# Making the prompt's keys and values between the last steps of the sample attention, with single waits in place of a meeting

## The reference

```python
q_lat = jnp.einsum("bthn,chn->bthc", q[..., :QK_NOPE], lw["w_uk"])
ckv = rmsnorm(ckv, lw["kv_norm_g"])
...
s = (einsum("bqhc,bkc->bhqk", q_lat, ckv) + einsum("bqhr,bkr->bhqk", q_pe, kpe)) * MLA_SCALE
s = where(k_pos <= q_pos, s, -inf)
o_lat = einsum("bhqk,bkc->bqhc", softmax(s), ckv)
yb = jnp.einsum("bthc,chv->bthv", o_lat, lw["w_uv"]).reshape(B, T, 512)
```

## Time and profile before

| | |
|---|---|
| median of 3 runs | 2403.9 us (2401.56 to 2406.0) |
| the profiled execution's own time | 2401.4 us |
| its span from the first to the last instruction | 2399.6 us |
| TensorE busy | 2265.4 us (94%) |
| VectorE busy | 1252.1 us (52%) |
| ScalarE busy | 894.1 us (37%) |
| GpSimd busy | 284.2 us (12%) |
| mean granted TensorE clock | 0.968 of full |

### The profile page before, as it was taken

The page is one execution under the profiler, slowest core; times in us unless marked ns, Lnnn a source line. Parts: engine busy times, 40 slices in busy tenths (PEclk is TensorE's granted clock), DMA queues, the critical chain, the costliest instruction groups (busy, mean ns, idle before and its releaser), DMA issues.

```text
span 2399.6 us, 43196 instructions
## 1 busy us (share of the span) xinstructions
PE 2265.4 (94%) x17458; PEld 2060.1 (86%) x17458; DVE 1252.1 (52%) x2038; ACT 894.1 (37%) x1626; POOL 284.2 (12%) x285
## 2 busy tenths in 40 slices
PE   7989998999998999999999999989999889999997
PEld 7966666699997899999888666667999888999996
DVE  4744443433457773566667444334333677626664
ACT  4334343433335431334343343334233354313333
POOL 0022220000015000000240222100000240000002
PEclk9989998899999999999999899988999999999998
DMA  6245550022252322225333455300223422322251
GB/s 223 79 148 172 171 179 1 1 72 86 79 170 75 96 86 93 70 79 174 113 108 107 148 178 173 125 1 11 87 80 98 153 80 88 102 76 73 85 186 51
DMA packets 68366, 250.40 MB, mean 104 GB/s; under 512 B 8272, under 2 KB 13264, under 8 KB 68112
## 3 DMA queue, kind: packets, MB, share of 16 engines
q1 hardware_dynamic: 45360, 164.79, 21.3%
q0 software_dynamic: 18432, 75.51, 9.7%
q10 hardware_dynamic: 4448, 8.33, 1.0%
HBM read 243.69 MB, written 4.90 MB: 104 GB/s over the span
## 4 chain that ended last, share of the span: by engine, by line
PE 83%; DVE 7%; issue 3%; POOLq 2%; ACT 2%; DMA 1%; DVEq 1%; another core or an unknown queue 0%; ACTq 0%; SPq 0%
PE PS L930 55%; PE PS L1123 5%; PE PS L1147 5%; PE PS L1167 5%; PE PS L1136 2%; DVE m_WL L1339 2%; POOLq L446 2%; PE PS L1276 1%; PE PS L1153 1%; PE PS L1254 1%; DVE m_X L1371 1%; DMA m_WS<-in_w_units 1%; PE PS L1265 1%; PE PS L961 1%; DVE m_XL L1379 1%
## 5 line engine op out<-in xcount | busy, mean ns | idle before, releaser
L930 PE MATMUL PS<-m_XH,m_WH 128*128 128x288 f32 x2560 | 734.9, 299 | 47.4 <-DVE m_WL L1339 29.5
L930 PE MATMUL PS<-m_XL,m_WH 128*128 128x288 f32 x2560 | 726.5, 297 | 0.0
L930 PE MATMUL PS<-m_XH,m_WL 128*128 128x288 f32 x2560 | 584.5, 298 | 0.0
L930 PEld LDWEIGHTS PS<-m_XH,m_WH 128*128 128x128 f32 x2560 | 487.1, 190 | 55.0 <-DVE m_WL L1339 37.0
L1339 DVE TENSOR_TENSOR m_WL<-m_WS,m_WH 128x1024 fp32r<-128x1024 f32 (+2 forms) x284 | 369.4, 1302 | 245.3 <-ACT m_WH L506 235.1
L930 PEld LDWEIGHTS PS<-m_XL,m_WH 128*128 128x128 f32 x2560 | 487.5, 190 | 0.8
L506 ACT ACTIVATE m_WH<-m_WS 128x1024 fp32r<-128x1024 f32 (+2 forms) x284 | 315.4, 1113 | 314.1 <-PE PS L930 293.6
L930 PEld LDWEIGHTS PS<-m_XH,m_WL 128*128 128x128 f32 x2560 | 425.7, 190 | 0.0
L930 PE MATMUL PS<-m_HH,m_WH 128*128 128x288 f32 x704 | 206.2, 300 | 5.5 <-DVE m_HL L1339 5.5
L930 PE MATMUL PS<-m_HL,m_WH 128*128 128x288 f32 x704 | 204.7, 299 | 0.0
L491 POOL DMA_INDIRECT m_RAW<-in_cache_rows,m_IDXS x128 | 122.6, 958 | 542.8 <-PE PS L1167 240.2
(11 more groups left out here) (274 smaller groups left out, 3216.9 us busy)
## 6 DMA issues: line engine op xcount, KB each, us to landing
m_WS<-in_w_units SPq DMA_DIRECT2D x232, 512.0 KB
m_WS<-in_w_units SPq DMA_DIRECT2D x48, 704.0 KB
m_WS<-in_w_units SPq DMA_DIRECT2D x4, 576.0 KB
out_y<-m_X SPq DMA_DIRECT2D x8, 288.0 KB, 2.2
m_RAW<-in_cache_rows,m_IDXS POOLq DMA_INDIRECT x128, 5.3
m_BRI<-in_branch_in ACTq DMA_DIRECT2D x2, 760.0 KB, 4.2
m_CST<-in_consts SPq DMA_DIRECT2D x1, 1425.5 KB, 13.5
m_X<-in_x_t SPq DMA_DIRECT2D x4, 288.0 KB, 7.8
```

The source lines that it names most:

```text
L930: mm = pe.matmul(out(half), w(part, k), x(k)[:, half_of(half)], start=(k == 0 and part == 0 and x is xh), stop=(k == last and part == 1))
```

## The change

Nothing is computed that was not computed before; the order changes, and some buffers move.

- Meeting 1 is gone. `N_MEET` is 2, and what waited for meeting 2 now waits for meeting 1.
- ScalarE splits off `WUKH` after step 29's exponentials and `WUVH` after step 30's; VectorE makes `WUKL` at the end of step 30 and `WUVL` at the end of step 31, after `accumulate(30)`.
- TensorE makes keys 0 and 1 before step 31's `turn_probs`, keys 2 and 3 between it and `values(31)`, in banks 2 to 5; value tiles 0 and 1 after `values(31)` in banks 6 and 7; after the swap value tiles 2 and 3 in banks 2 and 3, once VectorE has read keys 0 and 1 there; and only then the products with `DG`.
- VectorE makes `KNL` 0 and 1 after packing `CMB`, and `KNL` 2 and 3 between the differences `CDF` and the rest of the weights' chain.
- The samples' own values (`sample_values`, now in bank 7) follow the prompt attention's first scores.
- `DG` moves to the place of `PRB`; `WUKH` and `WUKL` move behind the last cache buffer.

```diff
-N_MEET = 3
+N_MEET = 2
...
-        DG = at("DG", [P, DB, NS], F32, r_z)
+        DG = at("DG", [P, DB, NS], F32, r_t)
...
+        o = max(o, r_xs + 2 * (RAWS - 1) * ROW * 4)
         WUKH = at("WUKH", [P, KT, 512], F32R, o); o += 4096
...
# ScalarE
                     exponentials(u)
+                    if u == NU2 - 3:
+                        act.wait_ge(S["wuk2_in"], (l + 1) * 16)
+                        copy(WUKH[:, :, :], WUK2[:, :, :]).then_inc(S["pre_hi"], 1)
+                    if u == NU2 - 2:
+                        act.wait_ge(S["wuv_in"], (l + 1) * 16)
+                        act.wait_ge(S["pv_mm"], CREDIT["pv_mm"] + l * NU2 + NU2 - 3)
+                        copy(WUVH[:, :, :], WUV[:, :, :]).then_inc(S["pre_hi"], 1)
...
+                prompt_keys(0)
                 probs(NU2 - 1)
+                prompt_keys(1)
+                prompt_keys(2)
+                prompt_keys(3)
+                copy(IDR[:, :], C["ident"])
...
+                prompt_values(0)
+                prompt_values(1)
                 act.wait_ge(S["cdf"], l + 1)
...
-                meet(act, "met_act", l, 1)
...
+                prompt_values(2)
+                prompt_values(3)
...
# TensorE
+                pe.wait_ge(S["pre_lo"], 2 * l + 1)
+                prompt_keys(0)
+                prompt_keys(1)
                 pe.wait_ge(S["s_exp"], (l + 1) * NU2)
                 turn_probs(NU2 - 1)
+                prompt_keys(2)
+                prompt_keys(3)
                 values(NU2 - 1)
+                pe.wait_ge(S["pre_lo"], 2 * l + 2)
+                prompt_values(0, 6)
+                pe.wait_ge(S["o_acc"], CREDIT["o_acc"] + (l + 1) * NU2)
+                prompt_values(1, 7)
                 pe.wait_ge(S["cmb"], l + 1)
...
+                for kt in (2, 3):
+                    pe.wait_ge(S["kn_lo"], l * 4 + kt - 1)
+                    prompt_values(kt, kt)
+                pe.wait_ge(S["kn_lo"], (l + 1) * 4)
                 pe.wait_ge(S["dg"], l + 1)
...
-                meet(pe, "met_pe", l, 1)
...
+                pe.wait_ge(S["v_ev"], l * 5 + 4)
+                pe.wait_ge(S["pre_hi"], 3 * l + 3)
...
+                    if u == 0:
+                        sample_values()
+                    if u == 2:
+                        pe.wait_ge(S["v_ev"], (l + 1) * 5)
...
# VectorE
+                    if u == NU2 - 2:
+                        dve.wait_ge(S["pre_hi"], 3 * l + 1)
+                        lo(WUKL[:, :, :], WUK2[:, :, :], WUKH[:, :, :]).then_inc(S["pre_lo"], 1)
+                    if u == NU2 - 1:
+                        dve.wait_ge(S["pre_hi"], 3 * l + 2)
+                        lo(WUVL[:, :, :], WUV[:, :, :], WUVH[:, :, :]).then_inc(S["pre_lo"], 1)
...
+                prompt_keys(0)
+                prompt_keys(1)
                 dve.wait_ge(S["sw_mm"], l + 1)
...
+                prompt_keys(2)
+                prompt_keys(3)
                 dve.wait_ge(S["cex"], l + 1)
...
-                meet(dve, "met_dve", l, 1)
```

More of the change, by code:

```diff
@@ L817, in _ @@
                     exponentials(u)
+                    if u == 0:
+                        act.wait_ge(S["v_mm"], l * 5 + 5)
+                        copy(YBT[0:NS, 4, :], PS[0:NS, 7, :]).then_inc(S["v_ev"], 1)
                     if u >= 1:
@@ L1196, in _, with prompt_keys, prompt_values @@
                     values(u - 1)
+                def prompt_keys(i):
+                    for ct in range(KT):
+                        c = slice(i * P, (i + 1) * P)
+                        mm = three(PS[:, 2 + i, :], WUKH[:, ct, c], WUKL[:, ct, c],
+                                   CKH[:, ct, 0:SEQ], CKL[:, ct, 0:SEQ], ct == 0, ct == KT - 1)
+                    mm.then_inc(S["kn_mm"], 1)
+                def prompt_values(kt, bank):
+                    for ct in range(KT):
+                        c = slice(kt * P, (kt + 1) * P)
+                        mm = three(PS[:, bank, :], CKH[:, ct, c], CKL[:, ct, c],
+                                   WUVH[:, ct, :], WUVL[:, ct, :], ct == 0, ct == KT - 1)
+                    mm.then_inc(S["v_mm"], 1)
+                pe.wait_ge(S["pre_lo"], 2 * l + 1)
+                prompt_keys(0)
+                prompt_keys(1)
                 pe.wait_ge(S["s_exp"], (l + 1) * NU2)
                 turn_probs(NU2 - 1)
+                prompt_keys(2)
+                prompt_keys(3)
                 values(NU2 - 1)
+                pe.wait_ge(S["pre_lo"], 2 * l + 2)
+                prompt_values(0, 6)
+                pe.wait_ge(S["o_acc"], CREDIT["o_acc"] + (l + 1) * NU2)
+                prompt_values(1, 7)
                 pe.wait_ge(S["cmb"], l + 1)
@@ L1208, in _, with sample_values @@
                     mm.then_inc(S["ol_mm"], 1)
-                meet(pe, "met_pe", l, 1)
[L1212 to L1224, removed]
-                    mm.then_inc(S["v_mm"], 1)
[L1226 to L1234, removed]
+                pe.wait_ge(S["v_ev"], l * 5 + 4)
+                pe.wait_ge(S["pre_hi"], 3 * l + 3)
+                def sample_values():
+                    pe.wait_ge(S["ols"], l * 2 + 2)
+                    for h in range(HEADS):
+                        c = slice(h * NS, (h + 1) * NS)
+                        for ct in range(KT):
+                            mm = pe.matmul(PS[0:NS, 7, c], OLS[:, ct, c], WUV[:, ct, c], start=(ct == 0), stop=(ct == KT - 1))
+                    mm.then_inc(S["v_mm"], 1)
                 def scores(u):
@@ L1296, in _ @@
                     mm.then_inc(S["yt_mm"], 1)
[L1297 removed]
+                meet(pe, "met_pe", l, 1)
                 with pe.Fori(0, DT) as i:
@@ L1714, in _ @@
                                 PS[:, 5, :].rearrange("p (b h t) -> p b h t", b=DB, h=HEADS)).then_inc(S["ols"], 1)
-                meet(dve, "met_dve", l, 1)
-                dve.wait_ge(S["pre_hi"], 3 * l + 1)
-                lo(WUKL[:, :, :], WUK2[:, :, :], WUKH[:, :, :]).then_inc(S["pre_lo"], 1)
-                dve.wait_ge(S["pre_hi"], 3 * l + 2)
-                lo(WUVL[:, :, :], WUV[:, :, :], WUVH[:, :, :]).then_inc(S["pre_lo"], 1)
-                for i in range(4):
-                    dve.wait_ge(S["kn_hi"], l * 4 + i + 1)
-                    lo(KNL[:, i, :], PS[:, i, :], KNH[:, i, :]).then_inc(S["kn_lo"], 1)
                 def maxima(u):
```

35 lines of the change are left out of this document (16 added, 19 removed).

## The result

| | before | after |
|---|---|---|
| median (range) | 2403.1 us, 4 runs (2401.56 to 2406.0) | 2372.0 us, 3 runs (2369.7 to 2373.53) |
| the profiled execution's own time | 2401.4 us | 2372.0 us |
| its span | 2399.6 us | 2370.2 us |
| TensorE busy | 2265.4 us (94%) | 2253.7 us (95%) |
| mean granted clock | 0.968 | 0.975 |

The time after is 0.987 of the time before, with a 95% interval of 0.985 to 0.989: 31.7 us, 27 to 36. (Two runs of the changed kernel, 2416.55 us here and 2423.78 us in a later group, ran at a lower mean clock, 0.954 and 0.953, and stand in none of the medians, ratios and means.) Forecast were 26.2 us and 2377.7.

A forecast was written before the change was run, and what follows sets the result against it. TensorE's path bounds the kernel, losing time in waits and at half clock where the sample attention ends. Stretches of 35.0 and 36.4 us become 22.6 each, 26.2 us off 2403.9: 2377.7, range 2372.5 to 2386.

The forecast's parts named there:

- what would show it: The prediction's list of signs expected in the changed profile: waits, clock at 1.00, both stretches 22 to 24 us, prompt attention unchanged.
- stall: TensorE's wait for the weights' chain before the products with `DG`: 0.96 us, in place of 1.10 + 2.61.
- scores and samples' values: End of the stretch: 4.41 us less the removed wait of 0.73, 3.68, plus 0.2 for turns between kinds of product.
- Rival 2: VectorE's or ScalarE's back-to-back PSUM copies cost 0.1 to 0.3 us more each; 2381 to 2383 us, chance 0.09.
- the estimate of 0.2 for turns: In the first scores and samples' own values: 0.2 us added for TensorE's turns from one kind of product to the other.
- The steps moved ahead: Weight splits moved into the last sample steps: costed at nothing; without cover up to 1.06 us on ScalarE, 0.16 on VectorE.
- Rival 1: The clock falls to half in the products with `DG`: 2382 us in one layer, near 2386 in both; chance 0.22.
- the row at 467 us: Profile row before the change: clock goes to half after narrow 128x64 products, TensorE busy 60.77 of 63 us; evidence for a fall.
- Rivals 3 and 4: 3: clock falls, stays half through prompt attention, 2484 us, chance 0.02; 4: time comes back elsewhere, near 2400, chance 0.02.
- the gain is taken from either: Whole kernel: the same 26.2 us subtracted from the profiled time, giving 2375.2, and from the median 2403.9, giving 2377.7.
- low end: Bottom of the range, 2372.5 us: no stall (1.9), no turns (0.4), 2.3 us for the runs' spread below their median.
- a further gain of 2 to 4 us: Case in which the stall and the 0.2 for turns vanish and the clock's phase is kind; chance 0.03.

## Why the prediction was right or wrong

**The mechanism: right.** The list under "what would show it" came nearly to the letter: no wait between `values(30)` and value tile 3, one wait before `DG`'s products, ended by VectorE's `DG`, of 0.70; the clock at 1.00 through both stretches; 21.98 and 21.93 us, a hair below the 22 to 24; the attention as long as before. The wait of 0.70 is at the low edge of its 0.7 to 1.5. The sample steps weren't longer (below).

**The terms of the stretch, layer 0, from the end of `values(30)`:**

| | forecast | measured |
|---|---|---|
| `values(31)` done | 8.13 | 8.06 |
| swap's start | 10.89 | 10.84 |
| value tile 3 done | 14.04 | 13.96 |
| `DG` ready | 15.00 | 14.66 |
| stall | 0.96 | 0.70 |
| `DG`'s products | 3.74 | 3.69 |
| scores and samples' values | 3.88 | 3.63 |
| second scores | 22.6 | 21.98 |

All are small and of one sign. The chain was 0.34 faster: a pair of `KNL` took 1.28 in place of 1.38, since two back to back overlap, where 0.69 had been counted for each; the differences were 0.16 earlier; and VectorE began the pair before the last difference had quite ended. Rival 2 had it the other way (back to back costs more) and is wrong. The 0.25 of the last term is nearly all the estimate of 0.2 for turns, which weren't there. It makes 0.6 per layer, 1.3 in all: 27.47 in place of 26.2. These terms were mis-sized, by little: had the runs gained just these 27.5 us, the median would have been 2376.4, well inside the range.

**The steps moved ahead cost nothing,** as counted. From `values(29)` to `values(30)` TensorE's rows are 6.84 us apart in a later profile of the kernel before (366.13 to 372.97, layer 0). In the kernel after, layer 0, `values(28)`, `values(29)` and `values(30)` start at 357.48, 364.33 and 371.17, so 6.85 with the split of `WUKH` between them and 6.84 with those of `WUVH` and `WUKL`. The gain was split between waits and the rest as forecast: 7.7 of 12.5 in waits, measured 7.95 of 13.03.

**Rival 1 did not come in the change, and could have.** Of 20 stretches in the profiles of kernels with the change's order up to `DG` (the change's ten, two of one-layer kernels, four with the early swap, two with the samples' values first, two with the meeting) the clock fell within `DG`'s products in one, at a price of 0.96 for the products there (in the four with the early swap no wait stands before them). So the row at 467 us was rightly taken as a warning; one fall in 20 stretches is a chance of near 0.1 for the two of a kernel, where 0.22 was given. Rivals 3 and 4 did not come: the window 395.05 to 454.00 of the kernel after is at clock 1.00, and the chain is at 83% on TensorE still.

**The step that failed** is the one that carries the sum over to the timed runs: "the gain is taken from either", 26.2 us off the profile's time and the same 26.2 off the median. It takes what the profiled executions save in the stretches for what the timed runs save, and puts the difference at nothing, without a reason. The low end, "no stall (1.9), no turns (0.4) and 2.3 us for the runs' own spread below their median", lets the stretches be shorter than forecast, but has no term for a median that gains more than they do; a further gain of 2 to 4 us had been given a chance of 0.03. Measured in its place: 27.5 us in the stretches and 31.5 ± 1.4 in the timed runs, so 4.0 us for the term that stood at nothing, against 1.3 for all the mis-sized ones.

What are these 4.0? The clock seems to be the smaller part. The runs' mean granted clock, 0.9684 before and 0.9751 after, makes 151.8 and 118.0 us at half clock, 33.8 less and so 16.9 ± 1.6 us of time, while the stretches alone had 31.6 us at half clock in the mean of four profiles (15.8); that leaves 1.1 ± 1.6 for the clock elsewhere. The excess seems to be in both layers (above). The profiled executions of before are all four faster than its timed mean, by 2.8 on average (2401.4, 2397.9, 2401.8, 2400.0 against 2403.1), and so is that of the kernel with only its buffers moved (2399.8 against 2404.9); those of the change are not (2372.8 on average against 2371.6). So the kernel before may well spend more in these stretches in the runs that leave no profile; that is an argument from leftovers, not shown, and **the cause of these 4 us, 2.8 standard errors from nothing, stays open.**

## What to carry to other kernels

Here a chain of small steps on other engines cost TensorE twice: in the wait (7.95 us of layer 0's gain) and in the half clock after it (5.08). Independent products that are needed anyway, put into the waits, took both away; useless ones took away only a part of the second, and held up what stands behind them. Look for them across a meeting: what stood behind it (splits, keys, values) needed nothing of what it waited for. When forecasting, take the stretch of before from several executions where the clock falls in it, since it took 35.0 to 36.4 us in four profiles, and leave room in the range for timed runs that gain more, or less, than the profiled stretches do.

## What the runs showed that was not expected

The clock can fall while TensorE is busy: to 0.77 in a window of 3.00 us with 3.00 us of 128x64 products (with the meeting put back; the window begins 0.9 us after a wait of 0.69 has ended), and to 0.53 in a window with 3.63 of 4.00 us busy, right after the prompt attention in the kernel after:

```profile
395.05:454.00 58.95, 57.61 (x422) 42.80 (x420) 27.98 (x78) 23.15 (x77) 0.00 (x0) 1.00 0.00 1
454.00:458.00 4.00, 3.63 (x14) 2.48 (x14) 1.25 (x3) 1.30 (x2) 0.00 (x0) 0.53 0.00 0
```

For the same instructions of the same kernel the clock falls earlier in one execution than in the next; the timeline of TensorE in a later execution of the kernel before (layer 0, then layer 1) shows it beside the 6.09 of the earlier trace rows:

```profile
382.46 7.09 PE L1206 MATMUL PS<-m_DG,m_OAC 128*128 128x64 f32 x32 [2.62 <-DVE m_DG L1709]
...
1567.22 7.09 PE L1206 MATMUL PS<-m_DG,m_OAC 128*128 128x64 f32 x32 [2.62 <-DVE m_DG L1709]
```

Stages that the change does not touch vary by more than the sum's error: the stage of the gates up to `w_out`, at full clock throughout, from its first product with `YH` to the first with `MH`, took 180.96 or 183.28 us in profiles of either kernel and in either layer, and 187.14 in one of the change, with TensorE busy all the time. What chooses between them is open.
